# Two transformer blocks on one core: three quarters of the MLP's down projection as products of seven blocks in place of eight

## The reference, cut to what matters

```python
    h = h + memory_cross_attention(u, mem_n, w_xq, w_xkv, w_xo)
    u = rms_norm(h, norm_mlp_g)
    h = h + jnp.square(jax.nn.relu(u @ w_mlp1)) @ w_mlp2      # 1024 -> 4096 -> 1024
    return rms_norm(h, final_norm_g)
# and then, in the second block
    h = rmsnorm(x, g_norm); proj = h @ w_in                   # values, av, pairs ...
```

## Time and profile before

| | |
|---|---|
| median of 3 runs | 1350.21 us (1350.08 to 1350.26) |
| span of the profiled execution | 1348.7 us; what lies around it is not in the page, the median is 1.5 us above it |
| TensorE busy | 1334.4 us, 99% |
| VectorE, ScalarE, GpSimd busy | 939.1 us, 586.7 us, 70.7 us |
| moved by DMA | 127.02 MB, mean 94 GB/s |

### The profile page before, as it was taken

One profiled execution on the slowest core, in us unless ns is written; L12 is line 12 of the kernel. 1 busy time (PEld: TensorE's weight loads), 2 busy tenths in 40 slices (PEclk: granted clock), 3 DMA queues, 4 the chain that ended last, 5 costly groups with the idle time before them and its releaser, 6 DMA issues.

```text
span 1348.7 us, 17627 instructions
## 1 busy us (share of the span) xinstructions
PE 1334.4 (99%) x6397; PEld 1094.9 (81%) x6397; DVE 939.1 (70%) x1503; ACT 586.7 (43%) x990; POOL 70.7 (5%) x60
## 2 busy tenths in 40 slices
PE   7999999999999999999999999999999999999998
PEld 6787777788888888888888888888888888888886
DVE  7868888885576543355445563599889988995685
ACT  7535655564555432114333344734333433333234
POOL 1000000102002000000013300000000000000000
PEclk9999999999999999999999999999999999999999
DMA  5333333243323333323333342323233223323332
GB/s 164 94 93 79 73 74 89 63 141 97 107 80 107 95 93 110 93 76 112 94 93 93 94 121 83 97 78 93 73 98 95 82 76 89 87 74 109 98 106 94
DMA packets 224104, 127.02 MB, mean 94 GB/s; under 512 B 21234, under 2 KB 214851, under 8 KB 224034
## 3 DMA queue, kind: packets, MB, share of 16 engines
q1 hardware_dynamic: 222418, 123.47, 31.9%
q10 hardware_dynamic: 1616, 2.62, 0.6%
...
## 4 chain that ended last, share of the span: by engine, by line
PE 97%; DVE 2%; ACT 1%; issue 0%; ACTq 0%; DVEq 0%
PE lin L668 26%; PE lin L671 26%; PE lin L672 26%; PE ob L1095 1%; PE sc L760 1%; PE sc L1051 1%; PE sc L1054 1%; PE sc L1055 1%; PE tr L773 1%; PE ob L797 1%; PE sc L784 1%; PE tr L1054 1%; PE lin L1054 1%; PE tr L1055 1%; PE lin L1055 1%; PE tr L1051 1%
## 5 line engine op out<-in xcount | busy, mean ns | idle before, releaser
L1719 DVE TENSOR_TENSOR wl<-raw,wh 128x1024 fp32r<-128x1024 f32 (+2 forms) x235 | 287.2, 1230 | 62.1 <-ACT wh L1228 57.7
L1228 ACT ACTIVATE wh<-raw 128x1024 fp32r<-128x1024 f32 (+2 forms) x235 | 238.8, 1022 | 134.9 <-DMA raw<-in_w_mlp_dram 44.2
L668 PE MATMUL lin<-uh,wh 128*128 128x512 f32 x624 | 249.8, 400 | 0.5 <-DVE ul L1791 0.4
L672 PE MATMUL lin<-uh,wl 128*128 128x512 f32 x624 | 243.2, 390 | 0.0
L671 PE MATMUL lin<-ul,wh 128*128 128x512 f32 x624 | 243.1, 390 | 0.0
L668 PE MATMUL lin<-vh,wh 128*128 128x512 f32 x512 | 202.6, 396 | 0.2 <-DVE te L2369 0.2
L671 PE MATMUL lin<-vl,wh 128*128 128x512 f32 x512 | 199.6, 390 | 0.0
L672 PE MATMUL lin<-vh,wl 128*128 128x512 f32 x512 | 199.3, 389 | 0.0
L668 PEld LDWEIGHTS lin<-uh,wh 128*128 128x128 f32 x624 | 117.2, 188 | 27.8 <-issue 4.4
L671 PEld LDWEIGHTS lin<-ul,wh 128*128 128x128 f32 x624 | 117.3, 188 | 25.1 <-issue 2.2
L672 PEld LDWEIGHTS lin<-uh,wl 128*128 128x128 f32 x624 | 117.1, 188 | 24.7
...
## 6 DMA issues: line engine op xcount, KB each, us to landing
raw<-in_w_in_dram SPq DMA_DIRECT2D x100, 512.0 KB, 3.8
raw<-in_w_mlp_dram SPq DMA_DIRECT2D x64, 512.0 KB, 4.0
raw<-in_w_out_dram SPq DMA_DIRECT2D x16, 512.0 KB, 3.7
raw<-in_w_xkv_dram SPq DMA_DIRECT2D x8, 512.0 KB, 3.7
raw<-in_w_proj_b_dram SPq DMA_DIRECT2D x8, 512.0 KB, 3.8
raw<-in_w_proj_a_dram SPq DMA_DIRECT2D x8, 512.0 KB, 3.7
xtok<-in_x_dram ACTq DMA_DIRECT2D x4, 512.0 KB, 5.0
raw<-in_w_mla_out_dram SPq DMA_DIRECT2D x4, 512.0 KB, 3.5
```

The source lines that it names most:

```text
L668: ins = pe.matmul(o, wh[:, slot, at], xh_, start=start, stop=False)
L672: return pe.matmul(o, wl[:, slot, at], xh_, start=False, stop=stop)
L1228: act.activation(wh[:, c.slot(4), 0:size], raw[:, c.slot(2), 0:size], ACT.Copy).then_inc(hi_made, 1)
L1719: dve.tensor_tensor(wl[:, c.slot(4), 0:size], raw[:, c.slot(2), 0:size], wh[:, c.slot(4), 0:size].bitcast(F32), ALU.subtract).then_inc(lo_ ...
```

## The change

The hidden width is worked through in four quarters of 1024. Each quarter's up projection has 8 jobs. In three quarters the down projection (512 tokens x 1024 hidden x 1024 outputs) is cut into 2 x 2 x 2 blocks and computed by seven block products in place of eight: tokens in two halves of 256, hidden tiles in even and odd ones, outputs in two halves of 512. That needs sums of activation blocks (`sums`, then high and low parts of them) and of weight blocks (`pair_sums` and the addition behind each lowering from chunk 8 on), and sums of the seven parts (`part`, `combine`). The products have tokens on the output partitions; each part of 6 matmuls (`seven_part`) goes to two banks. A quarter has 14 chunks and 12 loads of whole weight rows into four raw slots (`RAW_SLOTS`); the odd tile's second half is loaded first and the whole odd tile later again. In the first quarter ScalarE copies the finished parts out of PSUM, later VectorE adds them. During the last up projection TensorE turns the total back, four transposes per tile (`turn_acc`), and VectorE adds it to `h` (`turned_added`). The last quarter's down projection stays as jobs of 24 matmuls, one output tile each. The mask table moves into the phase `av`, its iota on GpSimd behind `h_added`; a few waits on own results use one common semaphore. The MLP is no longer in loops.

The core of the diff, indented less; the lines taken out are those of the MLP in the kernel above, and "..." marks what is left out:

```diff
@@ phases
 PHASES = [("latent", 6, 6), ("conv", 8, 8), ("mvalues", 1, 0), ("heads", 28, 28), ("mla_out", 4, 8), ("conv_out", 4, 8),
+  ("w_out", 12, 12), ("xq", 4, 4), ("xv", 4, 0), ("xo", 4, 8), ("up0", 8, 8), ("down0", 14, 0), ("up1", 8, 8),
+  ("down1", 14, 0), ("up2", 8, 8), ("down2", 14, 0), ("up3", 8, 8), ("down3", 8, 8), ("values", 8, 0), ("av", 8, 0),
@@ counting
+SEVENS = 3
...
+def seven_sum(u, kk, n):
+    return SEVEN_SUMS * u + (3 * kk + n if n < 4 else 12 + kk + 1)
@@ banks and sums
+RAW_SLOTS = (raw2[:], raw3[:], raw[:, 1, :], raw[:, 0, :])
...
+T2S = (vtok[:].rearrange("p q d -> p (q d)"), logit[:, 512:1024], trig[:], rbc[:])
+SF = first_turned[:].rearrange("p t x -> p (t x)")[:, 0:1024].rearrange("p (n t) -> p n t", n=4)
+PART_X, PART_Q, PART_P, PART_R = (sc[0], sc[1]), (sc[2], ob), (lin[0], lin[1]), (tr[0], tr[1])
...
+SUM_X1, SUM_P, SUM_X2, SUM_R2 = ((acc[:, n, 0, :], acc[:, n, 1, :]) for n in range(4))
+SUM_Q1, SUM_Q2, SUM_R1 = (acc5[:, 0, :], acc5[:, 1, :]), (nlog[:], bias[:]), (atok_flat, te[:])
+ACC_BLOCKS = ((SUM_X1, SUM_R2), (SUM_Q2, SUM_Q1))
@@ block.sync
+for q in range(4):
+    c, _ = phase(f"up{q}")
+    for m in range(DT):
+        if q and m < 2:
+            sp.wait_ge(sums_made, seven_sum(q - 1, 2 + m, 4))
+        load(c + m, a["w_mlp1"][0], q * FFQ + P * m, DT, P)
+    c, _ = phase(f"down{q}")
+    rows = a["w_mlp2"][0][q * FFQ:(q + 1) * FFQ, :]
+    if q == SEVENS:
+        for m in range(DT):
+            load(c + m, rows, P * m, DT, P)
+        continue
+    for r in range(SEVEN_LOADS):
+        if r < 2:
+            if q:
+                sp.wait_ge(lo_made, seven_lowered(q - 1, 8 + r))
+                sp.wait_ge(sums_made, seven_sum(q - 1, r, 4))
+            else:
+                sp.wait_ge(std_made, NORM_NO["mlp"] + 1)
+        elif r < 4:
+            sp.wait_ge(lo_made, c.static + r - 3)
+        else:
+            sp.wait_ge(lo_made, seven_lowered(q, r - 4))
+            if r % 2 == 0:
+                sp.wait_ge(sums_made, seven_sum(q, (r - 4) // 2, 3))
+        kk, odd = (r // 2, r % 2) if r < 8 else (r - 8, 1)
+        first, n = (512, 512) if r < 8 and odd else (0, 1024)
+        tile = 2 * kk + odd
+        sp.dma_start(RAW_SLOTS[r % 4][:, 0:n], rows[tile * P:(tile + 1) * P, first:first + n])\
+            .then_inc(SLOT_LANDED[r % 4], 16)
@@ block.gpsimd
...
+pool.wait_ge(h_added, DT)
 dint = atok[:].rearrange("p a b -> p (a b)").bitcast(I32)
 step(pool.iota(dint, [[-1, S]], base=S - P, channel_multiplier=1))
 pool.tensor_copy(dist[:], dint).then_inc(pool_made, 1)
...
+pool.wait_ge(table_made, 1)
+pool.affine_select(out=nlog[:], in_=nlog[:], compare_op=ALU.is_ge, fill=BIG, base=S - P,
+                   pattern=[[-1, S]], channel_multiplier=1).then_inc(pool_made, 1)
@@ block.tensor
+def seven_part(banks, left, k, weights, slot, half, first, last, signal):
+    at = slice(512 * half, 512 * half + 512)
+    high, low_ = left
+    for r in range(2):
+        tok = slice(k + r * P, k + (r + 1) * P)
+        ins = pe.matmul(banks[r][:], high[:, tok], wh[:, slot, at], start=first, stop=False)
+        if weights and r == 0:
+            ins.then_inc(chunk_entered, 1)
+        pe.matmul(banks[r][:], low_[:, tok], wh[:, slot, at], start=False, stop=False)
+        ins = pe.matmul(banks[r][:], high[:, tok], wl[:, slot, at], start=False, stop=last)
+        if signal:
+            ins.then_inc(part_ready, 1)
+def taken(u, n):
+    wait(pe, part_taken, SEVEN_PARTS * u + n)
+def seven(u):
+    c, j = phase(f"down{u}")
+    for kk in range(4):
+        even, odd = (fh[:, 2 * kk, :], fl[:, 2 * kk, :]), (fh[:, 2 * kk + 1, :], fl[:, 2 * kk + 1, :])
+        s2, s3 = ((sh[:, kk, n, :], sl[:, kk, n, :]) for n in range(2))
+        last = kk == 3
+        x, y = c + 2 * kk, c + (2 * kk + 1)
+        pe.wait_ge(f_low, 12 * u + 3 * kk + 3)
+        pe.wait_ge(lo_made, (x + 1).v())
+        if kk == 0:
+            if u:
+                taken(u - 1, 10)
+        seven_part(PART_X, even, 0, True, x.slot(4), 0, kk == 0, last, last)
+        if kk == 0:
+            if u:
+                taken(u - 1, 12)
+        seven_part(PART_Q, even, 256, False, x.slot(4), 1, kk == 0, last, last)
+        pe.wait_ge(lo_made, (y + 1).v())
+        if kk == 0:
+            evacuated(pe, j + -2)
+            evacuated(pe, j + -1)
+        seven_part(PART_P, s2, 0, True, y.slot(4), 0, kk == 0, last, last)
+        if kk == 0:
+            if u:
+                taken(u - 1, 14)
+            else:
+                pe.wait_ge(std_made, NORM_NO["mlp"] + 1)
+        seven_part(PART_R, s3, 0, False, y.slot(4), 1, kk == 0, last, last)
+    for g in range(2):
+        for kk in (2 * g, 2 * g + 1):
+            odd, s4 = (fh[:, 2 * kk + 1, :], fl[:, 2 * kk + 1, :]), (s4h[:, kk, :], s4l[:, kk, :])
+            w = c + (8 + kk + g)
+            pe.wait_ge(lo_made, (w + 1).v())
+            if kk == 0:
+                taken(u, 2)
+            seven_part(PART_X, odd, 0, True, w.slot(4), 0, kk == 0, kk == 3, kk == 3)
+            if kk == 0:
+                taken(u, 4)
+            seven_part(PART_Q, s4, 0, False, w.slot(4), 1, kk == 0, kk == 3, kk == 3)
+        w = c + (10 + 3 * g)
+        pe.wait_ge(lo_made, (w + 1).v())
+        if g == 0:
+            taken(u, 8)
+        for n in range(2):
+            kk = 2 * g + n
+            odd = fh[:, 2 * kk + 1, :], fl[:, 2 * kk + 1, :]
+            seven_part(PART_R, odd, 256, n == 0, w.slot(4), n, kk == 0, kk == 3, kk == 3)
+def turn_acc(f):
+    if f > 1:
+        pe.wait_ge(h_added, f - 1)
+    for q in range(QT):
+        block = ACC_BLOCKS[f // 4][q // 2]
+        ins = pe.transpose(tr[f % 2][:, q * P:(q + 1) * P], block[q % 2][:, (f % 4) * P:(f % 4 + 1) * P],
+                           ident[:])
+    ins.then_inc(part_ready, 1)
+def turns(m):
+    if m < 2:
+        return {}
+    if m < 6:
+        return {4: lambda: turn_acc(m - 2)}
+    return {2: lambda: turn_acc(2 * m - 8), 5: lambda: turn_acc(2 * m - 7)}
+for q in range(4):
+    c, j = phase(f"up{q}")
+    for m in range(DT):
+        if q and m < 2:
+            taken(q - 1, 5 + m)
+        if q == SEVENS and m in (2, 6):
+            taken(SEVENS - 1, SEVEN_PARTS + (8 if m == 2 else 16))
+        job(c + m, j + m, DT, uh, ul, before=tiles_of(u_low, U0["mlp"]) if q == 0 and m == 0 else None,
+            between=turns(m) if q == SEVENS else {})
+        if q == 0 and m == 3:
+            sum_total("mlp")
+    if q < SEVENS:
+        seven(q)
+c, j = phase("down3")
+for m in range(DT):
+    job(c + m, j + m, DT, fh, fl, before=tiles_of(f_low, 12 * SEVENS) if m == 0 else None)
@@ block.scalar
+def seven_split(c, u, v):
+    high, raw_ = wh[:, c.slot(4), :], RAW_SLOTS[seven_load(v) % 4]
+    if v in (10, 13):
+        kk = 2 * (v // 13)
+        act.wait_ge(sums_made, seven_sum(u, kk + 1, 4))
+        wait(act, chunk_entered, (c + -2).v())
+        act.activation(high[:, 0:512], T2S[kk], ACT.Copy)
+        act.activation(high[:, 512:1024], T2S[kk + 1], ACT.Copy).then_inc(hi_made, 1)
...
+    else:
+        if v < 8:
+            act.wait_ge(sums_made, seven_sum(u, v // 2, 2))
+        else:
+            act.wait_ge(SLOT_LANDED[seven_load(v) % 4], seven_landed(u, seven_load(v)))
+        wait(act, chunk_entered, (c + -2).v())
+        act.activation(high, raw_, ACT.Copy).then_inc(hi_made, 1)
...
+def up(q):
+    c, j = phase(f"up{q}")
+    for m in range(DT):
         split(c + (m + 2))
+        if q < SEVENS and m == 7:
+            split(c + 10)
         to(j + m, (ta, tb)[m % 2][:], ACT.Relu)
+        n = 256 if q < SEVENS and m % 2 == 0 else S
+        act.wait_ge(f_sq, DT * q + m + 1)
+        act.activation(fh[:, m, 0:n], (tc, td)[m % 2][:, 0:n], ACT.Copy).then_inc(f_high, 1)
+        if q < SEVENS and m % 2:
+            kk = m // 2
+            act.wait_ge(s_made, 4 * q + kk + 1)
+            act.activation(fh[:, m - 1, 256:512], SF[:, 0, :], ACT.Copy)
+            act.activation(sh[:, kk, :, :], SF[:, 1:3, :], ACT.Copy)
+            act.activation(s4h[:, kk, :], SF[:, 3, :], ACT.Copy).then_inc(s_high, 1)
+        if q == 0 and m == 3:
+            norm_std("mlp")
+for q in range(4):
+    up(q)
+    c, _ = phase(f"down{q}")
+    if q < SEVENS:
+        for v in range(3, 10):
+            split(c + v)
+        if q == 0:
+            part_copied(0, SUM_X1, PART_X)
+            part_copied(1, SUM_Q1, PART_Q)
+        split(c + 10)
...
+        continue
+    for m in range(DT):
+        split(c + (m + 2))
+        act.wait_ge(h_added, DT + m + 1)
+        wait(act, hsq_added, 2 * m + 1)
+        src = h[:, m, :]
+        gain_high(uh[:, m, :], src, both[:, m:m + 1])
+        act.activation(ta[:], src, ACT.Square).then_inc(hsq_made, 1)
+        act.activation(tb[:], src, ACT.Square, scale=col("final_norm_g", m)).then_inc(hsq_made, 1)
@@ block.vector
+def pair_sums(u, kk):
+    ra, rb = 2 * kk, 2 * kk + 1
+    even, odd = RAW_SLOTS[ra % 4], RAW_SLOTS[rb % 4]
```

(139 more changed lines are left out.)

264 lines of the change are left out of this document (110 added, 154 removed).

## The result

The changed kernel takes 1371.51 us (median of 4 executions, 1370.34 to 1373.74) against 1350.17 before: ratio 1.016, 95% interval 1.0146 to 1.0175. That is 21.3 us slower; 10.8 had been forecast. The profiled execution is the longest of the four: 1373.74, span 1372.0, so 23.3 above the span before.

A forecast was written before the change was run, and what follows sets the result against it. TensorE, busy 99%, was taken as the bound: -16.3 for removed matmuls, +3.5 transposes, +17.8 product waits, +5.4 last up quarter, +0.4 last down quarter gave +10.8 on 1350.2, so 1361.0 us; range 1347.5 to 1372.

The forecast's parts named there:

- Each wait named: TensorE's new MLP waits: 17.8 us in the three seven-block products, 5.4 in the last up quarter.
- ReLU 7: ScalarE's ReLU of up job 7, at T+3.25 to T+3.85; TensorE waits for its bank 1.3 us, 4.1 in product 0.
- the second part: Each product's second part waits for chunk 3, lowered at T+12.97, and starts at T+13.15: 3.7 us.
- second wait: In each of the three products, TensorE waits for chunk 3's lowering: 3.7 us each.
- the forecast's own 1356 to 1366: Whole kernel: range of the forecast case alone, around 1361.0 us, with chance 0.56.
- the wider range: Whole kernel: 1347.5 to 1372 us, leaving out the faster case and little above.
- a rival with 0.09: TensorE's clock falls in the new gaps, 2.7 us per half-speed stretch, up to 13: 1374 us; chance 0.09.
- The last down quarter: Lowerings slowed beside GpSimd's additions in the last down projection: +0.4 us, bounds 0 and 4.2.
- GpSimd's longer addition begins behind the one lowering: Last down quarter: with this order the lowering was taken as hardly slowed, so +0.4 us.
- The addition at 408.96: Earlier VectorE addition from PSUM, 0.69 us beside GpSimd's work, cited for little contention in the last down quarter.
- The weaker rule that the prediction cited: Shared SBUF interfaces, contention for Vector instructions with two SBUF inputs: about 4 us more in the last down quarter.
- The waits are shorter than laid out: Rival on VectorE's queue in the MLP: the removed matmuls win, 1337.4 us without any wait; chance 0.19.

The follow-up runs named there:

- five reorderings: Changed kernel with chunk 3 ahead, first pairs and ReLU 7 ahead, last up quarter's waits, last down quarter's split and lowering, and the reciprocal moved: 1339.9 us, ratio 0.9923.

## Why the prediction was right, and where it was not

**Direction and mechanism of the waits held.** Each wait named is in the trace, at its place, and TensorE waited 22.4 us in the MLP, over the 13 below which the prediction called itself wrong. From product 1 (start T = 553.99): ReLU 7 was laid out for T+3.25 and ran at T+3.63; the second part was to start at T+13.15 and did at T+13.54. VectorE's timeline there, low parts of the sums, third pair, and only then chunk 3:

```profile
562.86 0.42 DVE L2392 TENSOR_TENSOR fl<-first_turned,fh 128x256 fp32r<-128x256 f32 x1 [0.71 <-ACT s4h L1704]
...
564.14 0.68 DVE L1927 TENSOR_TENSOR raw<-raw 128x512 f32<-128x512 f32 x1
...
566.20 0.68 DVE L1943 TENSOR_TENSOR wl<-logit,wh 128x512 fp32r<-128x512 f32 x1
566.80 0.68 DVE L1944 TENSOR_TENSOR wl<-raw,wh 128x512 fp32r<-128x512 f32 x1
```

The waits sum to 20.4 against 23.2 forecast. Most of the miss is in product 0: its second wait was put at 3.7 and was 1.85, since a half-speed stretch had made TensorE later by 1.7.

**The size failed, by half.** 21.3 us came where 10.8 were forecast, outside the forecast's own 1356 to 1366. The median lies only 0.5 us inside the wider range, which ended at 1372, and two of the four executions (1372.2 and 1373.7) lie beyond it: that the range held was luck. 12.5 us of the profile's 23.3 were not in the sum: 8.4 of half speed, 2.3 in the last down quarter, 4.6 of small terms, less the 2.8 by which the waits were shorter. The step that failed is the clock. The prediction kept it as a rival with 0.09, five gaps of 3 us or more on top of the waits, 1374, and argued against it that "the new gaps are half as long, between dense stretches". Half the length was enough: four stretches, 8.4 us together, 1.7 in a product and about 3 in up 3, and the profiled execution took 1373.7. So the rival's mechanism is what happened, four stretches in place of five and 2.1 us each in place of 2.7. That its number fits too is partly luck: its clock term was 5 us too large, and the terms of the next paragraphs, which it did not hold, filled that up. The earlier trace rows had shown half speed behind 7.42 us of idle time and the waits of that trace held none between it and 0.4; a cost that nothing showed should have been bounded from both sides in the sum, from nothing to 2.7 for each gap, and was put at nothing.

**The last down quarter** was put at 0.4 with a bound of 4.2; it cost 2.75, and 0.9 more ahead of the values. The step was that "GpSimd's longer addition begins behind the one lowering". It begins 0.03 ahead of it, and then the lowering waits for it. Read again, say so: GpSimd's addition, at 697.02 just behind the start of the first lowering (696.92), was the long one (2.27), and then the second lowering was long; whichever starts second is held up. The addition at 408.96 reads one input from PSUM and the lowering both from SBUF, so it was a poor witness. The Trainium skill, SBUF — State Buffer, Who interferes with whom, has as its single rule that only the port pair which VectorE and GpSimd share causes contention, and that it is an exclusive lock; the order of issue decides who blocks. The trace agrees, 2.34 against 1.23 us for the lowering that starts second. The weaker rule that the prediction cited gave about 4 us more, near the 2.75 + 0.9 that came.

**Small terms**: restarts (0.16 each), 0.35 per product, the 0.56 ahead of product 0 and the 1.3 behind the MLP were not priced, and the transposes cost 0.475 a group. Two slips change nothing: GpSimd's second addition is 2.27 in the row, not 2.28, and 8 x 1.1 less 4.7 is 4.1, not 4.2. The loads never held TensorE, as forecast.

**The other rivals.** "The waits are shorter than laid out" was priced at 1337.4 without any wait. For the queues as written it was wrong; with five reorderings the same work takes 1339.9.
